# Transformer blocks on one core: forget-gate pairs with by-feature outputs, spread reciprocals and 64-row score tiles

## The chip, the cores and the metric

The kernel is one program on one core of a Trainium2 chip. Its time is the device time of one execution in microseconds. A core has a matrix engine (PE, with weight loads listed as PEld), a vector engine (DVE), a scalar engine (ACT), GpSimd (POOL) and queues that issue DMAs (SP is the one that streams the weights). The engines run side by side, each in its own order, and meet at semaphores.

## The reference, cut to what matters

Two transformer blocks follow each other on a 256 x 1024 activation in float32. The change lies in the token mixer of the first block, which has two kinds of attention heads. Eight "fox" heads of width 64 have a forget gate: a running sum of log forget values is added to the logits.

```
log_f = log_sigmoid(fgate + fox_forget_b)
c = cumsum(log_f, axis=1).transpose(0, 2, 1)
fox_o = causal_block_attention(fq, fk, fv, c)     # 8 heads of 64
...                                               # 4 "diff" heads, width 128 values
# causal_block_attention, for each 128-query block i:
s = einsum('bhqd,bhkd->bhqk', q[q0:q1], k[:q1]) * scale
s = s + c[q0:q1, None] - c[None, :q1]
s = where(mask, s, finfo.min); p = softmax(s)
outs.append(einsum('bhqk,bhkd->bhqd', p, v[:q1]))
...
m = concatenate([fox_o, diff_o]) @ w_out
x = x + rms_norm(m, mix_post_g)
f2 = swiglu(rms_norm(x, ffn2_pre_g), ...)         # the next FFN
```

So for 256 tokens each head has three 128 x 128 blocks of scores: two for the late queries (against both key blocks) and one for the early queries.

## The kernel before, in words

All large products are float32 products in three parts: an operand is split into a rounded high part and the rest (`three`, L660 to L666: high by high, high by low, low by high). The weights stream from HBM in pieces of 128 x 2048 numbers (1 MB) through a ring of three raw buffers. SP loads piece k once `lo_ready` says that the rest of piece k-3 has been computed (L538); it issues two DMAs of 512 KB. ACT rounds a piece (`hi`, L1363), DVE computes its rest (`lo`, L2002, or in two halves `half_lo`, L2008), and PE multiplies with it (`half`, L668). A unit of work on PE is one tile of `half`, three matmuls with 512 moving columns.

The token mixer works on pairs of heads, p = 0 to 3 diff, p = 4 to 7 fox (`pair`, L309). For one pair PE turns queries and keys (`turn_qk`), computes the scores (`scores`, L956), DVE finds the maxima (`maxima`), ACT takes the exponentials with their sums (`exps`), PE turns the weights (`turn_weights`), ACT and DVE copy them out of PSUM (`weights_out`), PE multiplies with the values (`values`), and DVE scales the outputs (`output`). The order is written out by hand for each engine in three functions with the name `diff_and_fox`; between the steps PE does units of products (`behind`, `products`), whose numbers stand in FOX_BEHIND. PE runs the scores of pair p+1 ahead of the turned weights of pair p.

For fox pairs the two heads have tiles of different height: head 0 uses rows 0 to 65 of the array (64 features, and two rows for the decay sum), head 1 uses all 128 rows, with zeros in the rows between. The scores of both heads of a pair lie in one bank for the late queries and one for the early ones. The turned weights are the stationary operand of the values, 64 value columns move. DVE scales four 128 x 64 outputs by their reciprocals into `proj`, rows by token. After the last pair PE turns those outputs (`fills(T_WOUT, ..., 2, 3)`, L1257, eight transposes), DVE scales and ACT and DVE split them, and then the remaining products of the output projection run.

The output projection has four pieces, N_WOUT to N_WOUT + 3: the first two for the diff half of the inputs, the last two for the fox half. Behind them come the pieces of the next FFN, N_FFN2 (49) and N_FFN2 + 1 (50), whose high and low parts have places of their own, but whose raw data go through the same ring. Piece 49 is loaded when the rest of N_WOUT + 1 (46) is done, piece 50 when that of N_WOUT + 2 (47) is. In `norms_between` DVE first computes the rest of piece 50 (L2084), and only then the normed and scaled sums that update x (`gained`, L2053, and `postnorm`, L2069); PE then turns x (`turn_x_half`, L731, the transposes at L717) for the next FFN.

Of the kernel before, what the change touches and what calls it, by code (L numbers as in the profile page):

```python
# [38 lines left out]
AUG = 64 + 2  # L39
FQ, FK, FV, DQ, DK, DV, MIX = (512 * n for n in range(7))  # L40
FOX_EVEN, FOX_ODD = 5120, 8192
# [21 lines left out]
DIFF_FIRST = [(0, 1), (1, 1), (0, 0), (1, 0)]  # L63
FILLS = [DIFF_FIRST if u == T_WOUT else BY_HALF if u in (T_FFN1, T_WOUT2) else BY_TILE for u in range(9)]

# [14 lines left out]
FOX_BEHIND = {4: (1, 2), 5: (1, 2), 6: (1, 1), 7: (0, 0)}  # L80
# [46 lines left out]
def build(nc, x_d, wg_d, wu_d, wd_d, win_d, wout_d, win2_d, whg_d, wat_d, wout2_d,  # L127
          fixed_d, rows_d, post_d, bias_parts_d, level_d, out_d, row_d, skew_d):

    with ExitStack() as ctx:  # L130
# [130 lines left out]
        attn_hi_ready, hg_kept = sem("attn_hi_ready"), sem("hg_kept")  # L261
        pT_full, pT_a, pT_d, pv_done, o_out = sem("pT_full"), sem("pT_a"), sem("pT_d"), sem("pv_done"), sem("o_out")
# [62 lines left out]
        def late_half(p, h):  # L325

            return gu[:, h, 0:S] if pair(p)[0] == 1 else late(p)[:, h * S:(h + 1) * S]

        def early_half(p, h):

            return gu[:, h, S:S + P] if pair(p)[0] == 1 else early(p)[:, h * P:(h + 1) * P]

        def late_both(p):

            return gu[:, :, 0:S] if pair(p)[0] == 1 else heads(late(p), 2)

        def early_both(p):

            return gu[:, :, S:S + P] if pair(p)[0] == 1 else heads(early(p), 2)

        def o_place(p, h, t):

            if pair(p)[0] == 0:
                return score_banks(p)[:, 1, S + (2 * h + t) * 64:S + (2 * h + t + 1) * 64]
            if pair(p)[0] == 1:
                return gu[:, 1 - t, 0:P]
            return gu[:, 0, (2 * h + t) * P:(2 * h + t + 1) * P]
# [47 lines left out]
        fox_q, fox_k = ([heads(proj[:, t, at:at + 4 * S], 4) for at in (FOX_EVEN, FOX_ODD)] for t in range(TT))  # L395
        decay_rows = xs[0:8, 1, 0:S]

        def fill_bank(u, i):

            if u == T_WOUT:  # L400
                return (gu if i < 2 else acc[:, 1, :, :])[:, i % 2, :]
            return {T_FFN2: acc[:, 1, :, :], T_WHG: acc[:, 1, :, :], T_WOUT2: gu}.get(u, tp)[:, i % 2, :]
# [44 lines left out]
        def turn_n(u):  # L447
            return 4 * u - (4 if u > T_WAT else 0)
# [210 lines left out]
        def _(pe):  # L659
# [8 lines left out]
            def half(k, r, banks, j, t, u=None, tiles=range(4), first_j=0, after_first=None):  # L668

                if t == 0 and tiles[0] == 0:  # L670
                    pe.wait_ge(lo_ready, k + 1 + 3 * r)
# [284 lines left out]
            def scores(p):  # L956
# [13 lines left out]
                if kind == 1:  # L970
                    at = [slice(64 * h, 64 * h + 64) for h in range(2)]
                    for h in range(2):
                        pe.matmul(late_half(p, h), q_sb[at[h], 0, P:S], k_sb[at[h], 0, :], start=True, stop=False,
                                  skip_group_check=True)
                    for h in range(2):
                        pe.matmul(early_half(p, h), q_sb[at[h], 0, 0:P], k_sb[at[h], 0, 0:P], start=False, stop=False,
                                  skip_group_check=True)
                    both = mask16.rearrange("p (o n) -> p o n", o=1).to_broadcast([P, 2, P])
                    for h in range(2):
                        mm = pe.matmul(heads(gu[:, h, P:3 * P], 2), id16[:, :], both, start=False, stop=True,  # L980
                                       skip_group_check=True)
                    mm.then_inc(scores_done, 1)
                    return
                for h in range(2):
                    rows_used = AUG if kind == 0 and h == 0 else P
                    if kind == 0:
                        q, k = (a[h][0:rows_used, i, :] for a in (fox_q, fox_k))
                    else:
                        q, k = q_sb[:, h, :], k_sb[:, h, :]
                    lt, el = late_half(p, h), early_half(p, h)  # L990
                    alone = kind == 2
                    pe.matmul(lt, q[:, P:S], k, start=alone or h == 0, stop=alone, skip_group_check=not alone)
                    mm = pe.matmul(el, q[:, 0:P], k[:, 0:P], start=alone or h == 0, stop=alone, skip_group_check=not alone)
                if kind == 0:
                    both = mask16.rearrange("p (o n) -> p o n", o=1).to_broadcast([P, 2, P])
                    pe.matmul(heads(late(p), 2)[:, :, P:S], id16[:, :], both, start=False, stop=True, skip_group_check=True)
                    mm = pe.matmul(heads(early(p), 2), id16[:, :], both, start=False, stop=True, skip_group_check=True)
                mm.then_inc(scores_done, 1)

            def turn_weights(p):  # L1000
                if pair(p)[0] == 1:
# [5 lines left out]
                    return  # L1007
                if pair(p)[0] == 2:
# [7 lines left out]
                    return  # L1016
                pe.wait_ge(exp_done, p + 1)
                for h in range(2):
                    for n in range(3):
                        mm = pe.transpose(turned[:, h, n * P:(n + 1) * P], e_sb[:, h, n * P:(n + 1) * P], idn)  # L1020
                mm.then_inc(pT_full, 1)

            def values(p):
                kind, i = pair(p)
                if p >= 2:
                    pe.wait_ge(o_out, p - 1)
                for h in range(1 if kind == 1 else 2):
                    wid = 64 if kind == 0 else P
                    col = (FV + i * P + 64 * h, DV + i * P, AV + i * S + h * P)[kind]
                    v = [proj[:, t, col:col + wid] for t in range(TT)]  # L1030
# [6 lines left out]
                    if p in (6, 7) and h == 1:  # L1037
                        pe.wait_ge(pT_d, p + 1)
# [10 lines left out]
            def diff_and_fox():  # L1049
# [42 lines left out]
                for p in range(4, 8):  # L1092
# [7 lines left out]
                    if p == 7:  # L1100
                        pe.wait_ge(o_out, 7)
                        half(N_WOUT + 1, 0, wout_banks(1), 1, 0, tiles=[0, 1], first_j=1)
                    pe.wait_ge(pT_a, p + 1)
                    if p < 6:
                        pe.wait_ge(pT_d, p + 1)
# [153 lines left out]
            filled(T_WOUT, 3)  # L1259
            for b in range(2):  # L1260
                half(N_WOUT + 2 + b, 0, wout_banks(b), 0, 0, first_j=1).then_inc(acc_bank, 1)
            filled(T_WOUT, 4)
# [92 lines left out]
        def _(act):  # L1355
# [150 lines left out]
            def q_out(p):  # L1506
# [4 lines left out]
                elif kind == 0:  # L1511
                    act.activation(fox_q[0][0:64, i, :], turned[0:64, 0, 0:S], ACT.Copy, scale=FOX_SCALE)
                    act.activation(fox_q[1][64:P, i, :], turned[64:P, 0, 0:S], ACT.Copy, scale=FOX_SCALE)\
                       .then_inc(qT_ready, 1)
# [4 lines left out]
            def exps(p):  # L1519
# [5 lines left out]
                if pair(p)[0]:  # L1525
# [8 lines left out]
                    return  # L1534
                for h in range(2):
                    lt, el = late_half(p, h), early_half(p, h)
                    n = 4 * (p % 2)
                    act.activation(e_sb[:, h, 0:S], lt, ACT.Exp, bias=nmx[:, n + h:n + h + 1], accum_out=den[:, h:h + 1])
                    last = act.activation(e_sb[:, h, S:3 * P], el, ACT.Exp, bias=nmx[:, n + 2 + h:n + 3 + h],
                                          accum_out=den[:, 2 + h:3 + h])  # L1540
                last.then_inc(exp_done, 1)

            def weights_out(p):
# [4 lines left out]
                n = S if pair(p)[0] == 1 else 3 * P  # L1548
                act.activation(pT_sb[:, 0, 0:n], turned[:, 0, 0:n], ACT.Copy).then_inc(pT_a, 1)

            def diff_and_fox():
# [54 lines left out]
                for p in range(4, 8):  # L1606
# [3 lines left out]
                    if p < 7:  # L1610
                        exps(p + 1)
                    if p == 4:
                        next_hi(N_WIN, 0, 23)

# [111 lines left out]
            hi(N_WOUT + 3)  # L1726
            fills(T_WOUT, 2, 3)
# [131 lines left out]
        def _(pool):  # L1859
# [43 lines left out]
            def odd_heads(a, one):  # L1903

                link(pool.memset(a[1][0:64, :, :], 0.0))
                link(pool.memset(a[1][0:2, :, :], one))

# [8 lines left out]
            odd_heads(fox_q, -1.0)  # L1916
            odd_heads(fox_k, 1.0)
# [20 lines left out]
            pool.dma_start(bass.AP(tensor=row_d.tensor, offset=0, ap=[[S, 8], [1, S]]), decay_rows).then_inc(aug_out, 16)  # L1938
            pool.wait_ge(aug_out, 16)
            for a, r in ((fox_q, 0), (fox_k, 1)):  # L1940
                for h, at in ((0, 64), (1, 0)):
                    pool.dma_start(a[h][at + r:at + r + 1, :, :], bass.AP(tensor=row_d.tensor, offset=h * S, ap=[[8 * S, 1], [2 * S, 4], [1, S]]))                        .then_inc(aug_in, 16)
# [46 lines left out]
        def _(dve):  # L1989
# [14 lines left out]
            def half_lo(k, b):  # L2004
# [5 lines left out]
                if b:  # L2010
                    ins.then_inc(lo_ready, 1)

# [188 lines left out]
            def k_out(p):  # L2201
# [4 lines left out]
                elif kind == 0:  # L2206
                    dve.tensor_copy(fox_k[0][0:64, i, :], turned[0:64, 1, 0:S])
# [655 lines left out]
```

## Time and profile before

| | |
|---|---|
| median of 3 runs | 992.8 us (992.78, 992.8, 995.76) |
| profiled execution, first to last instruction | 990.5 us |
| profiled execution, its own device time | not listed apart from its span; 2.3 us lie between the span and the median |
| PE, DVE, ACT, POOL busy | 986.0, 711.5, 486.3, 213.1 us |
| granted PE clock | full in all 40 slices |
| fox pairs | about 268.9 to 297 us of the span |

Times in the rows below are microseconds from the span's start. A row of the timeline gives the start, the length (of several merged instructions: from the first start to the last end), the engine, the line, the operation and the number of instructions. Each float32 matmul has two records. Matmuls overlap, so what one costs is the distance between starts, not its length.

### The profile page before, as it was taken

What the parts mean: (1) busy time and instruction counts of PE and PEld (TensorE: products, weight loads), DVE (VectorE), ACT (ScalarE), POOL (GpSimd) and SP (SyncE); (2) the same over time, 40 slices, a digit from 0 to 9 for tenths busy, and PEclk for the clock granted to TensorE, in tenths of its full rate; (3) what the DMA queues carried; (4) which work ended last, traced back from release to release, by engine and by line L of the source; (5) the groups of instructions that cost most, each with busy time, mean ns of one, the idle gap of its engine ahead of it and who ended that gap; (6) DMA issues with size and microseconds to landing.
All of it is one profiled execution on the core that took longest, in us unless ns stands there. A gap on an engine that the chain in (4) does not pass through costs nothing.

```text
span 990.5 us, 14542 instructions
## 1 busy us (share of the span) xinstructions
PE 986.0 (100%) x5302; PEld 835.5 (84%) x5302; DVE 711.5 (72%) x849; ACT 486.3 (49%) x621; POOL 213.1 (22%) x215
## 2 busy tenths in 40 slices
PE   9999999999999999999999999999999999999998
PEld 6888888888888888888888888888888888888887
DVE  6766666775788767676777998678875767667674
ACT  6534343664666543434545444365555445334342
POOL 3313232014100232323112600060000012223230
PEclk9999999999999999999999999999999999999999
DMA  9665656745425656565745625544536456556561
GB/s 316 224 212 169 212 169 214 253 131 190 129 85 170 209 173 210 171 205 177 247 154 174 204 94 200 188 145 147 168 121 220 130 184 230 172 178 201 179 210 42
DMA packets 121017, 178.53 MB, mean 180 GB/s; under 512 B 5760, under 2 KB 82112, under 8 KB 120848
## 3 DMA queue, kind: packets, MB, share of 16 engines
q1 hardware_dynamic: 120048, 174.86, 53.8%
q0 software_dynamic: 576, 1.39, 0.5%
q10 hardware_dynamic: 352, 1.73, 0.5%
q8 instruction: 27, 0.44, 0.2%
q14 instruction: 14, 0.11, 0.0%
HBM read 176.88 MB, written 2.64 MB: 181 GB/s over the span
## 4 chain that ended last, share of the span: by engine, by line
PE 99%; DMA 0%; SPq 0%; ACT 0%; issue 0%; DVE 0%
PE acc L662 11%; PE acc L666 10%; PE acc L665 10%; PE tp L863 10%; PE gu L863 10%; PE gu L868 5%; PE tp L868 5%; PE tp L662 4%; PE tp L666 4%; PE tp L665 4%; PE gu L662 3%; PE gu L665 3%; PE gu L666 3%; PE acc L1143 2%; PE acc L1146 1%; PE acc L1172 1%
## 5 line engine op out<-in xcount | busy, mean ns | idle before, releaser
L2002 DVE TENSOR_TENSOR wlo<-raw,whi 128x2048 fp32r<-128x2048 f32 x140 | 325.7, 2331 | 153.9 <-ACT whi L1363 152.4
L1363 ACT ACTIVATE whi<-raw 128x2048 fp32r<-128x2048 f32 x150 | 285.7, 1908 | 70.3 <-PE acc L666 22.7
L863 PE MATMUL tp<-act_in,whi 128*128 128x512 f32 x432 | 102.9, 390 | 0.0
L863 PE MATMUL gu<-act_in,whi 128*128 128x512 f32 x432 | 102.6, 390 | 0.0
L1899 POOL TENSOR_TENSOR tmp<-tmp 128x256 f32<-128x256 f32 x54 | 39.7, 736 | 275.8 <-DVE tmp L2123 275.8
L1901 POOL TENSOR_TENSOR sil<-sil,tmp 128x256 f32<-128x256 f32 x54 | 88.8, 1644 | 33.5 <-ACT sil L1434 33.5
L863 PEld LDWEIGHTS gu<-act_in,whi 128*128 128x128 f32 x432 | 80.9, 188 | 16.6
L662 PE MATMUL acc<-whi,hT_hi 128*128 128x512 f32 x240 | 94.0, 392 | 0.0
L665 PE MATMUL acc<-wlo,hT_hi 128*128 128x512 f32 x240 | 93.7, 390 | 0.0
L666 PE MATMUL acc<-whi,hT_lo 128*128 128x512 f32 x240 | 93.4, 389 | 0.0
L863 PEld LDWEIGHTS tp<-act_in,whi 128*128 128x128 f32 x432 | 79.8, 188 | 15.7
L1439 ACT ACTIVATE hT_hi<-hid 128x256 fp32r<-128x256 f32 x54 | 22.2, 417 | 137.1 <-DVE hid L2134 129.5
L1882 POOL TENSOR_SCALAR ms<-sums 128x1 f32<-128x1 f32 (+2 forms) x20 | 13.7, 685 | 270.3 <-ACT junk L1385 159.9
L1434 ACT ACTIVATE sil<-tmp 128x256 f32<-128x256 f32 x54 | 22.1, 408 | 101.3 <-POOL tmp L1899 101.3
L662 PE MATMUL tp<-whi,act_in 128*128 128x512 f32 x176 | 70.0, 398 | 0.0
L666 PE MATMUL tp<-whi,act_in 128*128 128x512 f32 x176 | 68.7, 390 | 0.0
L665 PE MATMUL tp<-wlo,act_in 128*128 128x512 f32 x176 | 68.6, 390 | 0.0
L868 PEld LDWEIGHTS gu<-act_in,wlo 128*128 128x128 f32 x432 | 55.4, 191 | 2.1
L868 PEld LDWEIGHTS tp<-act_in,wlo 128*128 128x128 f32 x432 | 55.4, 191 | 2.1
L868 PE MATMUL gu<-act_in,wlo 128*128 128x256 f32 x432 | 56.0, 283 | 0.0
L868 PE MATMUL tp<-act_in,wlo 128*128 128x256 f32 x432 | 56.0, 283 | 0.0
L666 PEld LDWEIGHTS acc<-whi,hT_lo 128*128 128x128 f32 x240 | 45.1, 188 | 9.6
(379 smaller groups left out, 1845.8 us busy)
## 6 DMA issues: line engine op xcount, KB each, us to landing
raw<-in_w_in SPq DMA_DIRECT2D x96, 512.0 KB, 4.7
raw<-in_down SPq DMA_DIRECT2D x66, 512.0 KB, 4.1
raw<-in_gate SPq DMA_DIRECT2D x64, 512.0 KB, 4.4
raw<-in_up SPq DMA_DIRECT2D x64, 512.0 KB, 4.9
raw<-in_w_out SPq DMA_DIRECT2D x16, 512.0 KB, 4.7
raw<-in_w_branch_hg SPq DMA_DIRECT2D x8, 512.0 KB, 4.3
raw<-in_w_branch_attn SPq DMA_DIRECT2D x8, 512.0 KB, 4.8
post<-in_post_gains SPq DMA_DIRECT2D x3, 512.0 KB, 6.2
```

What stands on the lines that cost most here:

```text
L662: pe.matmul(out, hi, w_hi, start=start, stop=False)
L665: pe.matmul(out, hi, w_lo, start=False, stop=False)
L666: return pe.matmul(out, lo, w_hi, start=False, stop=stop)
L863: pe.matmul(banks[:, a, :], w_hi[:, i, a * P:(a + 1) * P], both, start=i == 0, stop=False)
L868: mm = pe.matmul(banks[:, a, 0:S], w_lo[:, i, a * P:(a + 1) * P], act_in[:, i, 0, :], start=False, stop=i == KT - 1)
L1143: pe.matmul(banks[:, a, :], w_hi[:, i, a * P:(a + 1) * P], both, start=i == 0, stop=False)
L1363: act.activation(split_weights(k)[0], raw[:, k % RING, :], ACT.Copy).then_inc(hi_ready, 1)
L1434: act.activation(sil[:, a, :], gate[:, a, :], ACT.Silu).then_inc(sil_ready, 1)
L1439: act.activation(hT_hi[:, a, :], hid[:, a, :], ACT.Copy).then_inc(hT_hi_ready, 1)
L1899: pool.tensor_tensor(gate[:, a, :], gate[:, a, :], row, ALU.mult).then_inc(gate_scaled, 1)
L1901: pool.tensor_tensor(sil[:, a, :], sil[:, a, :], row, ALU.mult).then_inc(sil_scaled, 1)
L2002: dve.tensor_tensor(w_lo, raw[:, k % RING, :], w_hi.bitcast(F32), ALU.subtract).then_inc(lo_ready, 1)
```

## The change

- Scores of fox pairs: the 64 features of each head go into a 64-row tile of their own (rows 0 to 63 and 64 to 127, one bank per head), as the diff pairs already do. The decay sum goes in as four further bf16 matmuls with six rows each (three bf16 parts of the sum, and ones): POOL splits it into the three parts, and the DMAs that place it write six rows per head.
- Values of fox pairs: the values are the stationary operand (128 rows x 64 columns, one column half per head), the turned weights move (128 columns), and the output comes out by feature. It needs no turning: the eight transposes after the last pair, with their scaling, rounding and rests, are gone.
- The reciprocals are spread to 256 columns by a DVE copy, and turned by two more transposes per pair, behind the six of the weights. DVE multiplies the output with them in one instruction (`output`), ACT rounds the product (`fox_hi`), DVE computes the rest (`fox_lo`).
- The orders change: DVE finds all maxima of pairs 5 and 6 ahead of `k_out`, the reciprocals come ahead of the turned weights, the second half of the rest of piece N_WOUT + 1 moves back behind `weights_out(7)`, those of N_WOUT + 2 behind `output(7)` and `fox_lo`; ACT rounds N_WOUT + 3 ahead of `fox_hi(7)`; PE has FOX_BEHIND (2,1), (2,1), (2,0), (0,0) instead of (1,2), (1,2), (1,1), (0,0).

```diff
-FOX_BEHIND = {4: (1, 2), 5: (1, 2), 6: (1, 1), 7: (0, 0)}
+FOX_BEHIND = {4: (2, 1), 5: (2, 1), 6: (2, 0), 7: (0, 0)}
 # scores(p)
+                    if kind == 0:
+                        decay = [slice(64 * h, 64 * h + AUG) for h in range(2)]      # AUG = 6
+                        for h in range(2):
+                            pe.matmul(late_half(p, h), aug_q[decay[h], i, P:S], aug_k[decay[h], i, :], start=False,
+                                      stop=False, skip_group_check=True)
+                        for h in range(2):
+                            pe.matmul(early_half(p, h), aug_q[decay[h], i, 0:P], aug_k[decay[h], i, 0:P], ...)
 # turn_weights(p), fox
+                    pe.wait_ge(rden_ready, p + 1)
+                    for t in range(TT):
+                        mm = pe.transpose(turned[:, t, 3 * P:4 * P], fox_rden(p)[:, (1 - t) * P:(2 - t) * P], idn)
 # values(p), fox
+                    for h in range(2):
+                        pe.matmul(o[at[h], 0, :], v[0][:, at[h]], fox_pT[:, h, 0:P], start=True, stop=True, ...)
+                    for h in range(2):
+                        pe.matmul(o[at[h], 1, :], v[0][:, at[h]], fox_pT[:, h, P:S], start=True, stop=False, ...)
+                    for h in range(2):
+                        mm = pe.matmul(o[at[h], 1, :], v[1][:, at[h]], fox_pT[:, h, S:3 * P], start=False, stop=True, ...)
 # PE after the last pair
             diff_and_fox()
+            pe.wait_ge(lo_ready, N_WOUT + 2)
             half(N_WOUT + 1, 0, wout_banks(1), 1, 0, tiles=[2, 3], first_j=1)
-            pe.wait_ge(o_out, 8)
-            fills(T_WOUT, from_proj(MIX), 2, 3)
             half(N_WOUT + 1, 0, wout_banks(1), 1, 1, first_j=1)
+            pe.wait_ge(fox_lo_ready, 3)
+            half(N_WOUT + 2, 0, wout_banks(0), 0, 0, tiles=[0, 1, 2], first_j=1)
+            pe.wait_ge(fox_lo_ready, 4)
 ...
 # DVE, tail of diff_and_fox
                 output(5)
-                half_lo(N_WOUT + 1, 1)
-                reciprocals(6)
+                fox_lo(4)
+                fox_reciprocals(6)
                 maxima(7)
                 weights_out(6)
+                fox_lo(5)
                 output(6)
+                fox_reciprocals(7)
+                weights_out(7)
+                half_lo(N_WOUT + 1, 1)
+                output(7)
+                fox_lo(6)
                 half_lo(N_WOUT + 2, 0)
-                weights_out(7)
+                fox_lo(7)
                 half_lo(N_WOUT + 2, 1)
-                output(7)
```

## Rows read from the trace of the kernel before

**Rows 1.** The page: engines' busy time, and the chain that ended last.

```profile
PE 986.0 (100%) x5302; PEld 835.5 (84%) x5302; DVE 711.5 (72%) x849; ACT 486.3 (49%) x621; POOL 213.1 (22%) x215
PE 99%; DMA 0%; SPq 0%; ACT 0%; issue 0%; DVE 0%
```

**Rows 2.** Timeline of PE, fox pairs: scores, turned weights, values, units between.

```profile
275.88 0.60 PE L992 MATMUL gu<-proj 66*128 66x256 f32 x2
...
277.40 0.82 PE L1020 MATMUL acc<-fixed,att_e 128*128 128x128 f32 x6
278.20 0.47 PE L662 MATMUL acc<-whi,act_in 128*128 128x512 f32 x1
...
285.71 0.33 PE L1039 MATMUL gu<-proj,att_pT 128*128 128x64 f32 x2
...
286.97 0.48 PE L662 MATMUL acc<-whi,act_in 128*128 128x512 f32 x1
```

**Rows 3.** Timeline of PE, diff pair 0: scores in 64-row tiles.

```profile
233.36 0.40 PE L666 MATMUL acc<-whi,act_in 128*128 128x512 f32 x1
233.69 0.70 PE L973 MATMUL gu<-att_k,att_q 64*128 64x256 f32 x4
...
235.01 0.39 PE L665 MATMUL acc<-wlo,act_in 128*128 128x512 f32 x1
```

**Rows 4.** Timeline of PE, second block: products in two 64-column halves.

```profile
576.42 2.31 PE L1172 MATMUL acc<-proj 128*64 128x96 f32 x52
```

**Rows 5.** Waits of PEld, 215 to 345 us: total, times, longest.

```profile
PEld acc L953 <- ACT att_pT L1549: 1.5, 6, 0.4
```

**Rows 6.** Timeline of PE, DVE and ACT around the last fox pair.

```profile
289.98 0.82 PE L1020 MATMUL acc<-fixed,att_e 128*128 128x128 f32 x6
290.18 0.69 DVE L2236 TENSOR_REDUCE mx<-gu 128x2 f32<-128x512 f32 x1 [0.76 <-PE gu L997]
...
291.44 0.47 ACT L1538 ACTIVATE att_e<-gu,nmx 128x256 f32<-128x256 f32 x1
...
292.95 0.21 ACT L1539 ACTIVATION_READ_ACCUMULATOR att_e<-gu,nmx 128x1 f32 x1
...
293.51 0.82 PE L1020 MATMUL acc<-fixed,att_e 128*128 128x128 f32 x6
...
294.37 0.49 ACT L1549 ACTIVATE att_pT<-acc 128x384 f32<-128x384 f32 x1 [1.21 <-PE acc L1020]
...
295.56 0.33 PE L1039 MATMUL gu<-proj,att_pT 128*128 128x64 f32 x2
```

**Rows 7.** DVE prices: one line's instructions (min/median/max ns), and a timeline row.

```profile
L2205 DVE COPY att_k<-acc x4: 418/421/425, 232.4 to 258.4; 128x256 f32<-128x256 f32 x4
L2300 DVE RECIPROCAL rden<-den x4: 168/168/169, 278.7 to 295.3; 128x4 f32<-128x4 f32 x4
295.43 1.20 DVE L2008 TENSOR_TENSOR wlo<-raw,whi 128x1024 fp32r<-128x1024 f32 x1
```

**Rows 8.** Timeline of SP, DVE and PE, from piece 50's load to turned x.

```profile
296.65 0.37 SPq L540 DMA_DIRECT2D raw<-in_gate  x1
...
303.79 4.49 DVE L2002 TENSOR_TENSOR proj_rounded<-raw,proj_rounded 128x2048 fp32r<-128x2048 f32 x2
308.19 0.68 DVE L2053 SCALAR_TENSOR_TENSOR xs<-acc,post 128x512 f32<-128x512 f32 x1
...
310.77 0.60 PE L717 MATMUL acc<-fixed,x 128*128 128x128 f32 x4
```

**Rows 9.** Timeline around 790 us: a like pair of pieces ahead of the third FFN.

```profile
790.89 0.37 SPq L540 DMA_DIRECT2D raw<-in_gate  x1
...
793.09 0.92 SPq L540 DMA_DIRECT2D raw<-in_gate  x2
...
796.33 1.92 ACT L1363 ACTIVATE proj_rounded<-raw 128x2048 fp32r<-128x2048 f32 x1 [4.85 <-DMA raw<-in_up]
```

**Rows 10.** The page, DMA issues: count, size, median us from issue to landing.

```profile
raw<-in_gate SPq DMA_DIRECT2D x64, 512.0 KB, 4.4
```

More of the change, by code:

```diff
@@ L666, in three, with half @@
                 return pe.matmul(out, lo, w_hi, start=False, stop=stop)
-            def half(k, r, banks, j, t, u=None, tiles=range(4), first_j=0, after_first=None):
-                if t == 0 and tiles[0] == 0:
+            def half(k, r, banks, j, t, u=None, tiles=range(4), first_j=0, after_first=None, first_half=None):
+                if first_half is not None:
+                    pe.wait_ge(first_half, 1)
+                elif t == 0 and tiles[0] == 0:
                     pe.wait_ge(lo_ready, k + 1 + 3 * r)
@@ L984, in scores @@
                 for h in range(2):
[L985 to L997, printed above, removed]
+                    q, k = q_sb[:, h, :], k_sb[:, h, :]
+                    pe.matmul(late_half(p, h), q[:, P:S], k, start=True, stop=True)
+                    mm = pe.matmul(early_half(p, h), q[:, 0:P], k[:, 0:P], start=True, stop=True)
                 mm.then_inc(scores_done, 1)
@@ L1005, in turn_weights @@
                         mm = pe.transpose(turned[:, n // 2, n % 2 * P:(n % 2 + 1) * P], e_sb[:, 0, n * P:(n + 1) * P], idn)
+                    mm.then_inc(pT_full, 1)
+                    return
+                if pair(p)[0] == 0:
+                    pe.wait_ge(exp_done, p + 1)
+                    for h in range(2):
+                        for n in range(3):
+                            to = (n + 1) % 3 * P
+                            pe.transpose(turned[:, h, to:to + P], e_sb[:, h, n * P:(n + 1) * P], idn)
+                    pe.wait_ge(rden_ready, p + 1)
+                    for t in range(TT):
+                        mm = pe.transpose(turned[:, t, 3 * P:4 * P], fox_rden(p)[:, (1 - t) * P:(2 - t) * P], idn)
                     mm.then_inc(pT_full, 1)
@@ L1101, in diff_and_fox @@
                         pe.wait_ge(o_out, 7)
[L1102 to L1105, printed above, removed]
+                        half(N_WOUT + 1, 0, wout_banks(1), 1, 0, tiles=[0, 1], first_j=1, first_half=wout_first)
+                    weights_read(p)
                     if p < 6:
@@ L1547, in weights_out @@
                     act.wait_ge(pv_done, p)
-                n = S if pair(p)[0] == 1 else 3 * P
-                act.activation(pT_sb[:, 0, 0:n], turned[:, 0, 0:n], ACT.Copy).then_inc(pT_a, 1)
+                n = (4 * P, S, 3 * P)[pair(p)[0]]
+                to = pT_sb if pair(p)[0] else fox_pT
+                act.activation(to[:, 0, 0:n], turned[:, 0, 0:n], ACT.Copy).then_inc(pT_a, 1)
             def diff_and_fox():
@@ L1611, in diff_and_fox @@
                         exps(p + 1)
+                    else:
+                        hi(N_WOUT + 3)
                     if p == 4:
                         next_hi(N_WIN, 0, 23)
+                    fox_hi(p)
             def rounded_out(p):
@@ L1725, in _ @@
             diff_and_fox()
-            hi(N_WOUT + 3)
-            fills(T_WOUT, 2, 3)
             hi(N_FFN2)
@@ L2250, in weights_out @@
                     return
-                dve.tensor_copy(pT_sb[:, 1, :], turned[:, 1, 0:3 * P]).then_inc(pT_d, 1)
-                if pair(p)[0] == 0 and p != 6:
-                    reciprocals(p)
+                to, n = (pT_sb, 3 * P) if pair(p)[0] else (fox_pT, 4 * P)
+                dve.tensor_copy(to[:, 1, 0:n], turned[:, 1, 0:n]).then_inc(pT_d, 1)
             def late_reciprocals(p):
@@ L2294, in mix_rows, with fox_reciprocals, fox_lo @@
                                          op0=ALU.mult, op1=ALU.add).then_inc(mixed, 1)
-            def reciprocals(p):
+            def fox_reciprocals(p):
                 n = 6 * (p % 2)
                 dve.wait_ge(exp_done, p + 1)
-                dve.reciprocal(rden[:, n:n + 4], den[:, :]).then_inc(rden_ready, 1)
+                link(dve.reciprocal(rden[:, n:n + 4], den[:, :]))
+                dve.tensor_copy(heads(fox_rden(p), 4), per(rden[:, n:n + 4], 64)).then_inc(rden_ready, 1)
+            def fox_lo(p):
+                dve.wait_ge(fox_hi_ready, p - 3)
+                dve.tensor_tensor(heads(act_lo[:, p - 4, :], 2), fox_scaled(p), heads(act_hi[:, p - 4, :].bitcast(F32), 2),
+                                  ALU.subtract).then_inc(fox_lo_ready, 1)
             def output(p):
```

164 lines of the change are left out of this document (88 added, 76 removed).

## The prediction

> **What bounds the kernel now.** I read the page first: PE is busy for 986.0 of 990.5 us and the chain that ended last is 99% PE [rows 1]. So every instruction taken from PE counts, unless something else then becomes late. Next I read PE's timeline over the fox pairs for the distance from start to start, which is the price of a group; then the waits of its weight loads, which show how little it stands still; then the other engines between the last fox pair and the next FFN, because PE will get there earlier than now. The reader is to see there that a DVE chain ends just ahead of PE: PE turns x at 310.77 [rows 8], and one normal step of 0.23 us earlier it was still multiplying, so it hardly waited, but the data had been ready for only some 0.2 to 0.4 us.
>
> **PE's own work.** One group at a time:
>
> - Scores. Now 275.88 to 277.40, 1.52 us per pair [rows 2]. The diff pair shows the 64-row form with its masks: from the last product before it (233.36) to the second after it (235.01) are 1.65 us; two normal steps of 0.23 lie in that, so 1.19 [rows 3]. The four decay matmuls in bf16 (two of 256 columns, two of 128, six rows) are in no row. Four bf16 passes run two by two would cost about 0.16; run one after the other 0.33, and 0.2 more if PE has to stop twice for another tile height, so 0.53. I take 0.25, since heads in different rows did overlap in the diff pair. New price 1.44 (1.35 to 1.72), four times -0.08: **-0.3** (-0.7 to +0.8).
> - Values. Now 285.71 to 286.97 and 0.08 more, since the first product behind costs 0.31 instead of 0.23: 1.34 for 12 passes [rows 2]. The new form (64-column halves side by side) is like the second block's: 52 records of 96 columns in 2.31 us, 0.04 each [rows 4]. For 128 columns that scales to 0.053, times 12 = 0.64, with 0.1 for the change of form 0.75. Upper bound: no overlap, 0.11 a pass as now, 1.32. Saved 0.59 a pair, **-2.4** (-0.1 to -2.6).
> - Transposes. Eight added (two per pair), eight removed. Six are 0.82 long from the first start to the last end [rows 6], and one by itself 0.27, so a step is 0.11: 0.88 on both sides, **0**. But they move: 0.88 is added ahead of the last values and removed behind them.
> - Stalls of now that may go: 277.40 to 278.20 is 0.22 more than six transposes cost (PE waits for the diff half's rests) [rows 2]; the waits for the weights' copy held three times 0.2 or less in the fox pairs, of the six in the row [rows 5]. Together -0.5. Two units ahead of each such wait instead of one cover the second kind. The first stays: the spread reciprocals (0.5) come ahead of these rests on DVE, and the one 128x256 copy instead of two 64-row ones gives back 0.44, so the rests are ready at about the old time.
>
> Summed up, PE alone gives -2.7, up to -3.2 with the stalls. The products are the same in number.
>
> The Trainium skill (TensorEngine Tiling, Key Properties) says that changing the tiling mode, not just the tile, drains the engine. The trace agrees in part: the step into the 64-row tiles is 0.33 instead of 0.23 [rows 3]. By the rule the six-row matmuls would add a second change per pair, some 0.1 to 0.2 four times; this lies within the bounds above.
>
> **Where PE will wait.** I lay the steps out from the old slots. Scores of pair 6 come 0.56 earlier (281.6), those of pair 7 1.2 earlier (287.25), and PE wants the turned weights of pair 7 at 291.7 instead of 293.51 [rows 6]. Here a new wait opens, because one unit was moved ahead of values(6) and none is left behind it. Scores of pair 7 end at 288.7. Maxima start 0.2 later, the exponentials 1.26 after that, so 290.15, but ACT is in the copy of pair 6's weights: it starts 0.86 after six transposes begin, 0.22 later for eight (289.8), and takes 0.49, with 512 columns about 0.6: 290.4. The exponentials end 1.72 later [rows 6]: 292.15. PE waits about 0.5. The two last transposes wait for the spread reciprocals: output(6) ends on DVE at 292.4, reciprocal 0.17 with its own wait, then the copy, no row for one from SBUF, between 0.17 and 0.42 [rows 7]; I take 0.3: 293.0, PE goes on at 293.15, so 0.3 more. Then two transposes and two units: values(7) start at 294.8, against 295.56 now, 0.8 earlier only.
>
> **What sets the end: the load of piece 50.** Behind values(7) DVE has output(7) (its output is readable 1.0 after the start of the values, 295.8; product about 0.4), fox_lo(6) 0.37, half_lo of N_WOUT+2 1.17, fox_lo(7) 0.37, second half_lo 1.17 (1.20 with overlap, [rows 7]): it ends at 299.2 to 299.3. ACT isn't late: it rounds N_WOUT+3 before values(7) are out. Only then does SP load piece 50: now this was at 296.65 [rows 8]. So it is **2.6 us later, though PE is ahead**. Behind it DVE computes the rest of N_WOUT+3 for 2.2 us and so releases the next load 2.2 us after, the same spacing as at 790.89 and 793.09, where ACT idled until the data came and began 5.44 after the first issue [rows 9]. Add 1.95 for the rounding, 2.2 for the rest (half of 303.79 to 308.19), and 2.58 from `gained` to the turning of x (308.19 to 310.77), less 0.2 for what PE wasn't waiting for: 2.38 [rows 8]. 299.25 + 5.44 + 1.95 + 2.2 + 2.38 = **311.2, against 310.77 now: +0.4**. PE wants to turn x at 294.8 + 0.75 + 1.44 (two units) + 0.08 + 2.73 x 4 + 0.7 = 308.7, and stands still for 2.5 us. What follows (turned x, scaled, rounded, rest) hangs on this turning as it does now, so everything later moves by +0.4. Before, this transfer was hidden: DVE had two fills and then three rests to do, back to back until 308.19. Now DVE is early and the transfer is late.
>
> Bounds. The landing: 0.41 (between the two issues) + 4.4 = 4.8 for a piece alone [rows 10], 0.6 less. Values(7) without the two new stalls: 0.8 less. Decay and value matmuls at their upper ends: values(7) later by 0.8 x 3/4 + 0.57 x 3 = 2.3, less the 0.5 of stall that is then covered: 1.8 more. So the span changes by 0.4 - 1.4 = -1.0 to 0.4 + 1.8 = +2.2. Other edits are free: POOL splits the decay sum in five small operations and its DMAs move six rows instead of one, both 30 us ahead of the first fox scores; memsets in the setup are off every chain.
>
> My sum is made in the profiled execution, whose span of 990.5 is 2.3 below the median of the runs; I put the difference on the median: 992.8 + 0.4 = 993.2.
>
> **Rivals.**
> - A, PE's saving is kept. If DVE's tail frees piece 50 near 296.5 and PE never stops, the kernel gains PE's 2.7, at best 3.2: 990.1 (989.6). For it: DVE loses four 128x512 operations behind the last pair, and 72% busy looks roomy [rows 1]. Against it: the order puts five operations between output(7) and the load. Half kept (991.5) if the tail is 1.5 shorter than I have it.
> - B, the narrow tiles don't overlap, or six-row tiles cost a stop each. Values at 1.32 and scores at 1.72 cost +1.8 more at values(7), and with it at everything behind: 995.0. For it: no row shows these forms. Against it: the like forms do overlap [rows 3, 4]. It decides from about 1.0 us for a pair's values on.
> - C, the slower side by the clock. PE stands 2.5 us at the turning of x, far longer than the 0.4 of any wait in this stretch [rows 5], and the clock is full in all slices, so no row shows what such a gap does. If the granted clock falls to its lower level of 1.2 GHz there, each us of work at it costs a second one; for 3 us of work that is +3, so 996.2. It needs a gap at least as long as forecast. The Trainium skill (TensorE: Matmul & The Clock Gate, Why this matters for your kernels) warns of idle gaps of PE between bursts of matmuls; no row here shows whether this one is enough, and the chance is my estimate.
>
> **Chances.** My chain, within 1.2 of +0.4: 0.65. A whole or half: 0.17. B: 0.12. C: 0.06. What a measurement tells from no change is 0.3%, 3.0 us, so 989.8 and 995.8 are the limits. The chain lies inside. Of A only its best end reaches 989.8 (0.05 with the spread of the runs), of B and C 0.07. Faster 0.06, same 0.87, slower 0.07. The range is 991.2 to 994.9; for the chain alone 992.0 to 994.4.
>
> **What the changed profile would show.** Scores of a fox pair in about 1.44 and values in 0.75 from start to start; scores(7) near 287.3; a wait of PE ahead of the transposes of pair 7, and for the last two; the issue of piece 50's in_gate near 299.2 with ACT idle until about 304.7; a gap on PE of about 2.5 us before L717's transposes of x at about 311.2, and the same distance from there to the end as now. The prediction is wrong if piece 50 is issued before 298, if ACT isn't idle ahead of it, or if values take over 1.0.

## The result, and the profile after

| | before | after | ratio |
|---|---|---|---|
| first chip, median of 20 runs each | 995.58 us (992.61 to 996.28) | 998.0 us (992.59 to 1000.82) | 1.0028 [1.0015, 1.0041] |
| second chip, the same two kernels (18 and 6 runs) | 992.46 us (992.02 to 993.34) | 996.48 us (994.56 to 997.5) | 1.0034 [1.0022, 1.0046] |
| profiled execution, first chip: span | 990.5 us | 998.8 us (time 1000.57) | |
| profiled execution, second chip: span | | 995.7 us (time 997.5) | |

The forecast was +0.4 us, 993.2, with a range to 994.9. The medians differ by 2.4 us on the first chip (by the ratio 2.8) and by 4.0 on the second (by the ratio 3.4). The direction was right, the size and the range were not. On the first chip the kernel before itself came out at two levels, 7 of its 20 runs at 992.6 to 993.0 and 13 at 995.3 to 996.3; on the second chip it did not. So no experiment below is compared with runs of the first one: the first four ran on the second chip, the last four on a third, where the kernel before has the same median (992.46 us, 992.11 to 993.24, 33 runs). The kernel before has one profile only, from the first chip, in a run of its lower level.

The page of the kernel after first: engines' busy time and the chain that ended last. It answers to [rows 1].

```profile
PE 989.1 (99%) x5318; PEld 834.3 (84%) x5318; DVE 707.6 (71%) x835; ACT 485.3 (49%) x619; POOL 214.7 (21%) x218
PE 97%; DMA 1%; DVE 1%; ACT 0%; issue 0%; POOL 0%; SPq 0%; POOLq 0%
```

PE is busy for 3.1 us more, although the change took work from it: so some of its instructions ran longer. And the chain, 99% PE before, now runs 1% each through DMA and DVE. Next the waits of PE's weight loads from 215 to 345 us (total, times, longest), as in [rows 5]:

```profile
PEld acc L735 <- DVE x L2111: 5.2, 1, 5.2
...
PEld acc L971 <- ACT att_pT L1585: 0.8, 4, 0.2
...
PEld acc L1030 <- ACT att_e L1569: 0.3, 1, 0.3
...
PEld acc L1033 <- DVE proj L2334: 0.2, 1, 0.2
```

One wait stands out: the transposes of x for the next FFN, 5.2 us. It has no counterpart in [rows 5]. The others are as small as forecast.

To lay the two kernels side by side, cut the span at three marks: the first transposes of x in the whole kernel, those for the second FFN (lines 717 and 735), and the first matmul of that FFN with act_in as the weights (lines 863 and 881). In the kernel before these are at 10.33, 310.77 and 325.64; in the one after at 14.09, 317.56 and 333.90. Between the last mark and the end both take the same time within 0.3 us (as do all kernels below). So of the 8.3 us by which the spans differ, 3.8 lie ahead of the first mark, 3.0 between the first and the second, 1.5 between the second and the third. Ahead of the first mark the change touches only memsets of POOL in the setup, and no other profile of any of these kernels lies more than 0.8 behind the kernel before there. So only the last two, 4.5 us, belong to the change. On the second chip the changed kernel has its marks at 10.41, 314.12 and 330.98: +0.1, +3.3 and +2.0.

What the 3.8 are can be read in the same profile. PE starts on its first data at 5.20, against 4.34 before, and then goes from product to product in 0.42 us instead of 0.23, until 13.3. The same step of 0.42 stands behind PE's stop (318.90 to 319.32), where the granted clock is 0.57; here the view of the windows gives 1.00:

```profile
12.06 0.63 PE L779 MATMUL gu<-whi,act_in 128*128 128x512 f32 x1
12.48 0.63 PE L780 MATMUL gu<-whi,act_in 128*128 128x512 f32 x1
```

```profile
8.00:11.00 3.00, 3.00 (x10) 2.13 (x9) 1.06 (x3) 1.28 (x6) 0.00 (x0) 1.00 1.08 372
```

The fox pairs in the timeline of PE, kernel after, as in [rows 2] (start, length, line; subtract 3.8 for the late start):

```profile
279.45 0.40 PE L682 MATMUL acc<-whi,act_in 128*128 128x512 f32 x1
279.77 0.70 PE L992 MATMUL gu<-proj 64*128 64x256 f32 x4
280.31 0.39 PE L995 MATMUL gu<-proj 64*128 64x128 f32 x4
280.63 0.28 PE L1000 MATMUL gu<-proj 6*128 6x256 bf16 x2
280.75 0.22 PE L1003 MATMUL gu<-proj 6*128 6x128 bf16 x2
280.90 0.39 PE L1007 MATMUL gu<-mask,id 128*128 128x256 bf16 x2
281.13 0.82 PE L1030 MATMUL acc<-fixed,att_e 128*128 128x128 f32 x6
...
283.93 0.44 PE L1054 MATMUL tp<-proj 128*64 128x128 f32 x4
...
284.73 0.50 PE L678 MATMUL acc<-whi,act_in 128*128 128x512 f32 x1
285.07 0.39 PE L681 MATMUL acc<-wlo,act_in 128*128 128x512 f32 x1
```

From 279.45 to 281.13 are 1.68; less the last product's own 0.23 that is 1.45 for a pair's scores. The four decay matmuls take 0.27 (280.63 to 280.90). The values take 0.80 from first start to the next product, and that product costs 0.34 instead of 0.23; with 0.08 more ahead of them they come to 0.99.

Then the three engines that carry the chain into the next FFN, kernel after: SP's issues of pieces 49, 50 and 51, ACT's roundings of pieces 49 and 50, DVE's rest of piece 50 and the first sum for x, PE's last product and the transposes of x. In brackets stands the idle time before, and what ended it. It answers to [rows 8].

```profile
299.33 0.37 SPq L556 DMA_DIRECT2D raw<-in_gate  x1
303.08 0.37 SPq L556 DMA_DIRECT2D raw<-in_gate  x1
305.28 1.10 SPq L556 DMA_DIRECT2D raw<-in_gate  x2
```

```profile
305.27 1.92 ACT L1395 ACTIVATE proj_rounded<-raw 128x2048 fp32r<-128x2048 f32 x1 [4.71 <-DMA raw<-in_up]
311.12 1.91 ACT L1395 ACTIVATE proj_rounded<-raw 128x2048 fp32r<-128x2048 f32 x1 [3.93 <-DMA raw<-in_up]
```

```profile
313.06 2.29 DVE L2042 TENSOR_TENSOR proj_rounded<-raw,proj_rounded 128x2048 fp32r<-128x2048 f32 x1 [3.55 <-ACT proj_rounded L1395]
315.27 0.68 DVE L2095 SCALAR_TENSOR_TENSOR xs<-acc,post 128x512 f32<-128x512 f32 x1
```

```profile
312.40 0.39 PE L682 MATMUL tp<-whi,act_in 128*128 128x512 f32 x1
317.56 1.12 PE L735 MATMUL acc<-fixed,x 128*128 128x128 f32 x4 [4.77 <-DVE x L2111]
```

Piece 50 is asked for at 303.08, and ACT, idle for 3.93 us, starts on it at 311.12: **8.04 us from issue to use**. DVE, idle too, computes the rest and only then the sums; PE stands still for 4.8 us. Its transposes are then 1.12 long where they were 0.60 in [rows 8]. Last, the windows: length, busy time of PE, PEld, DVE, ACT, POOL (instructions), granted clock, DMA share, GB/s.

```profile
300.00:312.00 12.00, 12.00 (x55) 9.92 (x54) 7.55 (x7) 3.22 (x3) 0.00 (x0) 1.00 0.90 285
317.00:321.00 4.00, 3.44 (x13) 3.00 (x14) 2.76 (x5) 1.21 (x3) 0.00 (x0) 0.57 0.55 222
321.00:325.00 4.00, 4.00 (x20) 3.25 (x19) 3.04 (x7) 2.78 (x6) 1.00 (x2) 1.00 0.00 0
```

While pieces 49, 50 and 51 are fetched the DMA engines are 90% busy, and behind PE's stop the granted clock is 0.57 for 4 us, near the lower of its two levels (1.2 of 2.4 GHz), and full again from 321. That is the second part of the loss. The Trainium skill (TensorE: Matmul & The Clock Gate, Why this matters for your kernels) warns of idle gaps between bursts of matmuls. Here the trace agrees, with 4.8 us idle ahead and 0.57 behind.

### The profile page after: what moved, and what is told of

It reads as the page before. It is cut to its first block, busy times and chain, and to the rows that moved or that the text cites. A ratio compares the mean times of both kernels' runs of the same rounds, so it can differ in the third digit from the quotient of the medians.

```text
span 998.8 us, 14557 instructions
## 1 busy us (share of the span) xinstructions
PE 989.1 (99%) x5318; PEld 834.3 (84%) x5318; DVE 707.6 (71%) x835; ACT 485.3 (49%) x619; POOL 214.7 (21%) x218
## 4 chain that ended last, share of the span: by engine, by line
PE 97%; DMA 1%; DVE 1%; ACT 0%; issue 0%; POOL 0%; SPq 0%; POOLq 0%
PE acc L678 10%; PE acc L682 10%; PE acc L681 10%; PE tp L881 10%; PE gu L881 10%; PE gu L886 5%; PE tp L886 5%; PE tp L678 4%; PE tp L682 4%; PE tp L681 4%; PE gu L678 3%; PE gu L682 3%; PE gu L681 3%; PE acc L1175 2%; PE acc L1178 1%; PE acc L1204 1%
```

## The experiments

My theory after this result: piece 50's load, released late by the order on DVE, alone sets the end; its transfer is stretched because piece 49 is still under way and piece 51 is asked for right behind; and the long stop lowers the clock. The rivals: the new forms on PE cost more than they save (B of the prediction); the clock alone carries the loss; or transfers take longer in some executions by themselves, whatever stands beside them.

Each result below is a median with its range, and the ratio to the kernel before on the same chip.

**The changed kernel again (again)**, for the profile on the second chip.

> The changed kernel itself, once more, against the kernel before on the same chip. Theory L (late piece): ahead of the transposes of x for the second FFN PE stops for 3 to 5 us, because the raw data of piece 50 are issued 2.6 us later than before and then share the queues with pieces 49 and 51; the granted clock falls in that stop, which costs 1 to 2 us more. Ratio to before 1.002 to 1.004. Rival S (start): the whole difference is the start of the kernel, where the profiled run of the changed kernel lost 3.8 us before anything that was changed; then the ratio is 0.998 to 1.000 on another chip, and a stop at the transposes of x of under 1 us is seen.

Measured: 996.48 us (994.56 to 997.5), 1.0034 [1.0022, 1.0046]. SP asks for piece 50 at 299.49, ACT starts at 307.68, 8.19 later; the transposes of x in the timeline of PE:

```profile
314.12 1.11 PE L735 MATMUL acc<-fixed,x 128*128 128x128 f32 x4 [4.93 <-DVE x L2111]
```

The loss is there on a second chip, with the first mark in its usual place: rival S is out. The window behind PE's stop has a granted clock of 0.50:

```profile
314.00:318.00 4.00, 3.88 (x13) 3.31 (x14) 2.76 (x6) 1.21 (x3) 0.00 (x0) 0.50 0.47 190
```

All its six runs have a granted clock of 0.996 to 0.998 over the span; all 11 of the next kernel have 1.0.

**The rests put early (early_rests).** Only the order on DVE is changed.

```diff
                 output(5)
-                fox_lo(4)
+                half_lo(N_WOUT + 1, 1)
                 fox_reciprocals(6)
+                fox_lo(4)
                 maxima(7)
 ...
                 fox_reciprocals(7)
+                half_lo(N_WOUT + 2, 0)
                 weights_out(7)
-                half_lo(N_WOUT + 1, 1)
+                half_lo(N_WOUT + 2, 1)
                 output(7)
                 fox_lo(6)
-                half_lo(N_WOUT + 2, 0)
                 fox_lo(7)
-                half_lo(N_WOUT + 2, 1)
```

> One part undone: the rests of the weights come as early as DVE has room, the second half of N_WOUT + 1 behind output(5) as in the kernel before, the halves of N_WOUT + 2 around weights_out(7) instead of behind output(7) and fox_lo. Theory L: piece 50 is issued some 3 us earlier counted from the last pair's values, the stop ahead of the transposes of x falls from 5 to under 1 us, the clock stays full, and what PE saves in the fox pairs is kept: 1.5 to 2 us below before, ratio 0.998. Rival S: no difference to the changed kernel. Rival T (the tail's own cost): the copy of the last pair's weights comes 0.2 to 1.2 us later behind the half put ahead of it, and the ratio stays at 1.000 or above although the stop is gone.

Measured: **990.77 us** (990.4 to 991.62), 0.9983 [0.9974, 0.9992]. It beats both kernels: 5.7 us under the changed one, 1.7 under the one before. Its timeline: SP's issues of pieces 49 and 50, ACT's rounding of 50, PE at x.

```profile
289.35 0.37 SPq L556 DMA_DIRECT2D raw<-in_gate  x1
...
296.92 0.37 SPq L556 DMA_DIRECT2D raw<-in_gate  x1
```

```profile
303.27 1.92 ACT L1395 ACTIVATE proj_rounded<-raw 128x2048 fp32r<-128x2048 f32 x1 [3.79 <-DMA raw<-in_up]
```

```profile
309.49 0.39 PE L682 MATMUL tp<-whi,act_in 128*128 128x512 f32 x1
309.72 0.66 PE L735 MATMUL acc<-fixed,x 128*128 128x128 f32 x4
```

Piece 50 is asked for at the old time (296.65 in [rows 8]), PE goes from product to transposes in one step, and the clock stays full. All of the loss is gone, and the forms on PE are the same: so rival B is out, and the order is the cause. The edit puts piece 49's load and piece 50's early together; which of the two matters more, it doesn't tell.

**Piece 51 held back (hold51).**

```diff
                 if k >= RING:
                     sp.wait_ge(lo_ready, k - RING + 1 + 3 * r)
+                if k == N_FFN2 + 2:
+                    sp.wait_ge(hi_ready, N_FFN2 + 2)
```

> One wait added: SP issues piece 51 only when ACT has rounded piece 50, so that piece 50 doesn't share the queues with the piece behind it. Theory L with sharing: piece 50 lands about 5 us after its issue instead of 8, the stop ahead of the transposes of x falls to 2 to 2.5 us (what was forecast), ratio 0.999 to 1.001. Rival M (slow memory, not sharing): it still takes 7 to 8 us and the stop is as long as in the changed kernel.

Measured: 995.57 us (993.19 to 997.06), 1.0032 [1.002, 1.0044]. In its profile SP asks for pieces 50 and 51 at

```profile
299.85 0.37 SPq L558 DMA_DIRECT2D raw<-in_gate  x1
...
307.34 0.92 SPq L558 DMA_DIRECT2D raw<-in_gate  x2
```

and ACT and PE follow with

```profile
305.33 1.92 ACT L1397 ACTIVATE proj_rounded<-raw 128x2048 fp32r<-128x2048 f32 x1 [1.98 <-DMA raw<-in_up]
```

```profile
311.78 0.66 PE L737 MATMUL acc<-fixed,x 128*128 128x128 f32 x4 [2.22 <-DVE x L2113]
```

The piece is in use 5.48 after its issue instead of 8.2, PE's stop is 2.2 us, the clock over 309 to 314 us is full, and the second mark lies 300.9 behind the first, against 300.4 before: +0.5, where I had forecast +0.4. But this is the profiled run, 993.38 us, one of the two with a full clock (the other 993.19). The four with 0.998 took 995.23 to 997.06. So the short landing is seen in one trace of a quick run, while the medians (995.57 against 996.48) don't tell the two kernels apart, and the ratio lies outside the 0.999 to 1.001 that I expected. That piece 51 lengthens the landing is not shown by this run.

**Unused matmuls in the stop (warm)**: 16 of them ahead of the wait for x, none of their results is used.

```diff
             half(N_WOUT + 3, 0, wout_banks(1), 0, 1, tiles=[0], first_j=1)
+            for _ in range(16):
+                pe.matmul(heads(turned[:, 0, :], 4), id16[:, :], ...)       # 512 columns, bf16
             turn_x_half(T_FFN2, 0)
```

> Sixteen bf16 matmuls of 512 columns on the identity, into a bank that the next transposes overwrite, stand ahead of the wait for x (about 3.5 us of PE work whose result is not used). Theory L with the clock: the wait ends when it did, but the clock stays full behind it, so the kernel gains the 1 to 1.5 us that the slow stretch costs, in the runs in which the stop is longer than 3.5 us, and loses up to 1 us in others. Rival: if the clock falls by itself or at another place, the stretch behind the wait is as slow as in the changed kernel and the time doesn't fall.

Measured: 995.52 us (994.57 to 996.58), 1.0033 [1.0021, 1.0045], granted clock 1.0 in all six runs. The profile shows the filler and x behind it:

```profile
308.90 3.63 PE L1298 MATMUL acc<-id 128*128 128x512 bf16 x16
312.97 0.66 PE L735 MATMUL acc<-fixed,x 128*128 128x128 f32 x4 [0.45 <-DVE x L2114]
```

The transposes are short (0.66), and from x to the third mark 14.90 us pass, as before (14.87) and against 16.86 in again. So the lower clock's 2.0 us are saved in this trace, the quickest of the six runs. The median is 1.0 lower, which is not resolved (ratios 1.0033 and 1.0034, intervals nearly the same). But 3.1 us of loss stay with a full clock in every run. The clock alone does not carry the loss: the late data does, and in the traces the clock comes on top.

**Both (hold51_warm)**: the wait of hold51, and 10 unused matmuls.

> hold51 with ten matmuls whose result isn't used ahead of the wait for x (2.2 us of PE work, less than the stop of 2.6 us there). The runs of hold51 lay between 993.2 and 997.1 us. Theory K (clock): in the long ones the granted clock fell in the stop, so with PE kept busy all runs lie within 1 us of 993.2. Rival M (transfers): the long ones come from pieces that land at different times, and the spread stays at 3 us or more.

Measured: 994.78 us (992.74 to 997.12), 1.0022 [1.0013, 1.0031]; the clock full in 10 of 11 runs, and those 10 still spread from 992.74 to 995.57. So theory K fails, and the spread isn't the clock's: rival M forecast it. In its profile (993.67 us, the second quickest of 11) the landing is 6.24 us. Landings of varying length are what is left of the two causes named; one trace for each kernel can't show them.

**The kernel before with late loads (before_late)**: two waits on SP, nothing else changed.

```diff
                 if k >= RING:
                     sp.wait_ge(lo_ready, k - RING + 1 + 3 * r)
+                if k == N_FFN2:
+                    sp.wait_ge(pT_d, 8)
+                if k == N_FFN2 + 1:
+                    sp.wait_ge(turn_scaled, scaled_n(turn_n(T_WOUT) + 2))
```

> The harm alone, in the kernel before: SP issues piece 49 only when the last pair's weights are out (about 295.5 us instead of 289.4) and piece 50 only when the third fill is scaled (about 299.6 instead of 296.7), which is what the changed order does to them; nothing else is changed, so PE saves nothing. Theory L: piece 50 lands at 306 or later, PE stops 1 to 3 us ahead of the transposes of x, ratio 1.001 to 1.004. Rival (the late transfers are hidden): no stop, ratio 1.000.

Measured: 993.99 us (993.6 to 994.57), 1.0014 [1.0005, 1.0023]. The waits of PE's weight loads, and ACT's rounding of the piece asked for at 299.84:

```profile
PEld acc L721 <- DVE x L2073: 1.9, 1, 1.9
```

```profile
306.05 1.92 ACT L1367 ACTIVATE proj_rounded<-raw 128x2048 fp32r<-128x2048 f32 x1 [2.93 <-DMA raw<-in_up]
```

The cause works without any of the change's arithmetic: piece 49 asked for at 295.68 instead of 289.36 and piece 50 at 299.84 instead of 296.65 open the same stop at the same place, and cost 1.5 us. It costs less than in the changed kernel, because PE comes to x later there and because the landing takes 6.2 us; here piece 51 isn't asked for before 304.05.

**x ahead of piece 50 (x_first)**: ACT and DVE do what updates x first, and piece 50 afterwards.

```diff
                     acc_sums(m, 0, 1)
+                if m == 1:
+                    hi(n1 + 1)
 ...
-            hi(N_FFN2 + 1)
 ...
                 else:
-                    lo(n1 + 1)
+                    if m != 1:
+                        lo(n1 + 1)
 ...
                     fill_rest(u, 1)
+                    if m == 1:
+                        lo(n1 + 1)
```

> In the changed kernel ACT rounds piece 50 only behind the two sums of the output projection's first half, and DVE computes its rest only behind the turned x's second rest, so that the update of x doesn't queue behind piece 50. The loads come as late as in the changed kernel. Theory L (order within DVE): the stop ahead of the transposes of x falls from 5 us to under 1, and a new one opens where PE wants piece 50's rest, some 5.6 us behind, of about 2 us; ratio 0.999 to 1.002. Rival (something else than piece 50's rest holds x): the stop stays at 3 us or more.

Measured: 992.76 us (992.51 to 994.62), 1.0005 [0.9996, 1.0014]. The stop at x is gone (309.48), although the piece lands as late as ever (issue 299.93, rounding at 307.93): x was held only by piece 50's rest ahead of it on DVE. A new stop opens at the products of piece 50:

```profile
PEld gu L678 <- issue: 2.2, 1, 2.2
```

This one isn't made by the late load. ACT has rounded the piece by 309.85, and DVE, in the order of this experiment, comes to its rest only at 314.71, behind other work:

```profile
307.93 1.92 ACT L1395 ACTIVATE proj_rounded<-raw 128x2048 fp32r<-128x2048 f32 x1 [0.97 <-DMA raw<-in_up]
```

```profile
314.10 0.69 DVE L2071 TENSOR_TENSOR act_in<-tmp,act_in 128x512 fp32r<-128x512 f32 x1
314.71 2.29 DVE L2043 TENSOR_TENSOR proj_rounded<-raw,proj_rounded 128x2048 fp32r<-128x2048 f32 x1
```

The timeline of PE behind this stop:

```profile
314.94 0.39 PE L682 MATMUL gu<-proj_rounded,act_in 128*128 128x512 f32 x1
317.14 0.56 PE L678 MATMUL gu<-proj_rounded,act_in 128*128 128x512 f32 x1 [1.82 <-DVE proj_rounded L2043]
...
318.35 1.05 PE L735 MATMUL acc<-fixed,x 128*128 128x128 f32 x4
```

The new stop is half as long as the old one, and the kernel is 2.0 us above early_rests (992.76 against 990.77). Three of its 11 runs, the profiled one (994.5) among them, have a clock of 0.998 and took 994.46 to 994.62; the others, with a full clock, 992.51 to 993.28. In the profile PE idled for 1.8 us, and the transposes behind it are slow (1.05), while the 2.2 us of idle PE in hold51 left them at 0.66.

**Units spread otherwise (early_units)**: early_rests with one unit of products moved from ahead of the values of pair 5 to behind those of pair 6.

```diff
-FOX_BEHIND = {4: (2, 1), 5: (2, 1), 6: (2, 0), 7: (0, 0)}
+FOX_BEHIND = {4: (2, 1), 5: (1, 1), 6: (2, 1), 7: (0, 0)}
```

> early_rests with FOX_BEHIND (2,1), (1,1), (2,1), (0,0): one unit of products moves from ahead of values(5) to behind values(6), where PE waited 0.5 us for the last exponentials. The step of the forecast that this unit opened a wait: the wait ahead of the last pair's transposes goes, another of about 0.2 us comes ahead of turn_qk(7), and PE reaches the transposes of x 0.2 to 0.3 us earlier than in early_rests; ratio 0.998. Rival: the exponentials move with PE and nothing is gained, or the time rises by 0.2 us.

Measured: 990.78 us (990.44 to 991.68), 0.9983 [0.9973, 0.9992], no gain over early_rests. The two small waits at pair 7's weights (0.3 and 0.2) are gone, and the transposes of x start 298.65 us behind the first mark in both kernels, where I had expected 0.2 to 0.3 less. One wait of about the same size opens earlier instead, ahead of `turn_qk(7)`:

```profile
PEld acc L971 <- ACT proj L1585: 0.6, 1, 0.6
```

## Why the prediction was wrong

The account on the second chip, between the profiles again and early_rests there and the one profile of the kernel before: PE's saving -1.8 (the second mark lies 298.65 behind the first in early_rests, 300.44 before), the late x +5.1 (303.71 against 298.65), the clock +2.0 (16.86 against 14.87), together +5.3 for spans that differ by 5.2.

- **PE's own work: forecast -2.7, measured -1.7.** Scores 1.45 against 1.44 forecast, decay matmuls 0.27 against 0.25, the spread copy 0.29 against 0.3: right. The values came to 0.99, not 0.75. I had scaled the second block's 96-column passes (0.04 each, [rows 4]) by columns to 0.053; with 128 columns they take 0.80 / 12 = 0.067, and the change of form costs 0.19 on both sides together, not 0.1. A pair saves 0.35 instead of 0.59. (The -1.8 of the account also holds the waits that came and went.) This miss hardly moved the time, since piece 50 and not PE sets the end; but 0.99 is only just under the 1.0 from which B was to decide. The prediction weighed a rule of the Trainium skill (TensorEngine Tiling, Key Properties): a change of the tiling mode drains the engine. The trace shows a price and not its reason: 0.1 us per change into or out of the 64-column halves, and 0.27 for all four six-row matmuls with theirs.
- **Waits at pair 7: right.** 0.3 and 0.2 (forecast 0.5 and 0.3); values(7) start at 295.0 after the late start is taken off, forecast 294.8.
- **The load of piece 50 issued 2.6 later: right.** 303.08 - 3.76 = 299.3, forecast 299.25; the second chip has 299.49. PE wanted x at 308.9, forecast 308.7.
- **The step that failed: "began 5.44 after the first issue".** It is 8.0 and 8.2 in the two traces of the changed kernel. I took 5.44 from [rows 9], where piece 50's counterpart has one piece behind it. I counted what was issued behind it, and not what was issued ahead: piece 49 too had moved, from 289.36 to 299.33 (295.6 with the late start taken off; `half_lo(N_WOUT + 1, 1)` moved back), and was 3.75 us old. So piece 50 had piece 49 beside it until that landed (rounding at 305.27), and from 305.28 on piece 51. Over the kernels with traces, from issue to rounding: 8.04, 8.19, 8.00 (x_first) and 7.17 (warm) where 49 is 3.75 us ahead and 51 is 2.2 behind; 5.48 and 6.24 where 49 is as near but 51 is held for over 7 us; 6.2 in before_late, with 4.2 on both sides; 6.35 and 5.28 where 49 is 7.6 ahead and 51 3.4 to 3.8 behind. The two groups don't overlap. The missing 2.6 and 2.75 us go into x one for one. That the landing was this long is shown. That the neighbours made it so is argued from these traces, one execution each: both traces with piece 51 held come from quick runs of their kernels, and the medians of hold51 don't bear it out. That the transfers vary by themselves stays as a rival; no experiment moved piece 49 alone.
- **The clock was treated as a side case.** I gave C 0.06 and "+3 for 3 us of work", as an alternative to the main chain. It isn't one: it comes with the same stop. With the stop at 5 instead of 2.5 us it added 1.5 and 2.0. Of the 20 runs on the first chip 3 have a full clock, and they took 992.59 to 993.62, which is where the forecast of 993.2 lies; the 17 others, at 0.996 to 0.998, took 994.78 and more. No profile shows one of the 3, so why they came out there is open.
- **The range.** It took in PE's bounds on both sides, but of the landing only the lower one (4.8); no upper one was set, and the clock stood apart. With the landing and the clock put in as measured the main case would be 0.4 + 2.75 + 2.0 = +5.2, which is what the spans on the second chip differ by.
- **The base.** The median of the kernel before on the first chip turned out 2.8 us above the 992.8 on which I put the difference; one of the three given times, 995.76, hinted at it. So 2.8 of the 4.8 us between the forecast and 998.0 are the base, and 2.0 the rest.

The failed step in one sentence: the landing of piece 50 was put at 5.44 us and took 8.0 and 8.2, and the clock behind the longer stop, left out of the main case, added 1.5 and 2.0.

Rival A (the saving is kept) would have needed the load near 296.5, and early_rests shows that this is what happens when it is: 990.8, within its 989.6 to 991.5. B is out. C's mechanism is there, together with the main chain.

Left open: why runs of one kernel with this stop differ by 2.0 (warm) and 2.8 us (hold51_warm) even at a full clock, and what made PE slow at the start of the profiled execution on the first chip. That this start, 3.8 us, and the upper level of the kernel before, 3 us, are the same thing is possible; no profile of the kernel before at that level shows it.

## What to carry to other kernels

When a step is moved back, list all loads that it releases, and place them on a time axis with the loads ahead and behind: a transfer's time from a place where it is alone, or has one neighbour, need not hold where it has one on either side, so give it an upper bound too. A shorter PE makes a late load worse, so a saving on PE and the release of the next weights have to be moved together: with the same arithmetic the order made the difference between +4.0 and -1.7 us. If a stop of PE opens, price the clock behind it as part of the same case.

## What the runs showed of the hardware

- Transfers of 1 MB in pairs of 512 KB: from issue to use 5.3 to 6.4 us in the five traces with a neighbour further off on at least one side, 7.2 to 8.2 in the four with three pieces asked for within 6 us (in the first of them 285 GB/s and a DMA share of 0.90 over 12 us). One execution each.
- The clock's reaction is no function of the stop's length alone: 2.2 us of idle PE left it full in hold51, 1.8 us lowered it in x_first (0.57 over the next 4 us), 1.4 us left it full in before_late, 4.9 us lowered it to 0.50 over the next 4 us in the changed kernel on the second chip.
- A granted clock of 1.00 in the view does not rule out a slow PE: at the start of the changed kernel's first profile the products take 0.42 us a step instead of 0.23 beside it.
- Two-pass float32 matmuls in 64-column halves with 128 moving columns take 0.067 us a pass, against 0.11 for whole tiles with 64 moving columns: this is a gain of 40%, not of a half.
